# A 768-column slice of an expert table read as a stream, the other 1280 columns gathered, and a second row product per group on GpSimd

## What is computed

```
scores = einsum(q, keys)                       # 8 heads x 2 halves x 128 keys
idx, gate = top 16 of 16 x 16 sums per head    # idx = i * 128 + j, 128 experts a token
hid = gelu(einsum('td,thkd->thk', x, U[idx]))  # U: 16384 x 2048
out = einsum('thk,thkd->td', gate * hid, V[idx])
x = rms_norm(x + out)
```

## Time and profile before

| | |
|---|---|
| median of 3 runs | 2047.74 us (2046.32, 2047.74, 2051.26) |
| span of the profiled execution | 2047.2 us |
| projections | 0 to 884 us |
| first table, 63 groups after the first | 886 to 1515 us |
| tail, tile 1 | 1515 to 1564 us |
| second table and output | 1564 to 2047 us |
| busy share of the span | PE 70%, DVE 79%, ACT 42%, POOL 49% |

### The profile page before, as it was taken

How to read it: one execution, slowest core, us unless ns; L and a number is a source line. 1 busy time by engine, 2 the same in 40 slices (tenths; PEclk the granted TensorE clock), 3 DMA queues, 4 the chain that set the end, 5 groups by cost and what they waited for, 6 DMA issues and landing times.

```text
span 2047.2 us, 22565 instructions
## 1 busy us (share of the span) xinstructions
PE 1436.2 (70%) x7933; PEld 1248.8 (61%) x7933; DVE 1608.7 (79%) x1995; ACT 868.3 (42%) x1130; POOL 994.3 (49%) x699
## 2 busy tenths in 40 slices
PE   6999999999999999920000002212359999999997
PEld 6987998877888789920000001111247888888886
DVE  5465775454755556789999999977889999999998
ACT  4353443344343444311211226567856444444444
POOL 1002320000000000178888888888888788888862
PEclk9999999999999999965555555555569999999999
DMA  5555434444555555789999999999965999999996
GB/s 207 185 185 185 157 132 144 142 156 155 195 184 185 187 184 176 277 346 407 418 417 415 419 400 421 414 422 414 421 244 195 389 386 390 398 406 390 390 384 235
DMA packets 151803, 601.81 MB, mean 294 GB/s; under 512 B 14720, under 2 KB 14736, under 8 KB 118288
## 3 DMA queue, kind: packets, MB, share of 16 engines
q0 software_dynamic: 58048, 364.41, 44.0%
q1 hardware_dynamic: 93648, 236.02, 32.2%
HBM read 598.29 MB, written 2.10 MB: 293 GB/s over the span
## 4 chain that ended last, share of the span: by engine, by line
PE 55%; DVE 16%; issue 14%; POOL 7%; DMA 6%; ACT 2%; DVEq 0%; POOLq 0%; SPq 0%; ACTq 0%
PE acc L1715 7%; PE acc L1716 7%; PE acc L1717 7%; DVE slots L1470 6%; POOL slots L537 5%; PE acc L1698 4%; PE acc L1700 4%; PE acc L1701 4%; PE acc L2021 3%; PE scr L2022 3%; PE acc L2022 3%; DMA v_raw<-in_v_dense 3%; PE scr L2021 3%; PE scr L2023 3%; PE acc L2023 3%
## 5 line engine op out<-in xcount | busy, mean ns | idle before, releaser
L951 DVE TENSOR_TENSOR w_lo<-raw,w_hi 128x2048 fp32r<-128x2048 f32 x136 | 314.6, 2314 | 281.8 <-ACT w_hi L606 280.7
L1470 DVE SCALAR_TENSOR_TENSOR slots<-slots,acc 128x2048 f32<-128x2048 f32 x188 | 424.6, 2284 | 44.0 <-DMA slots<-in_peer_u,expert 41.7
L606 ACT ACTIVATE w_hi<-raw 128x2048 fp32r<-128x2048 f32 x136 | 260.1, 1913 | 409.0 <-PE acc L1717 263.3
L560 POOL DMA_INDIRECT starts<-in_v_gather,expert x256 | 365.1, 1426 | 92.9 <-DVE X L1620 77.7
L537 POOL DMA_INDIRECT slots<-in_peer_u,expert x256 | 250.2, 977 | 241.9 <-DVE expert L1442 145.2
L545 POOL TENSOR_TENSOR slots<-slots,N 128x2048 f32<-128x2048 f32 x62 | 280.5, 4524 | 37.2 <-DMA slots<-in_peer_u,expert 37.1
L887 ACT ACTIVATE v_hi<-v_raw 128x1344 fp32r<-128x1344 f32 x128 | 170.5, 1332 | 260.5 <-PE scr L2023 202.7
L800 ACT ACTIVATE slots<-slots 128x2048 f32<-128x2048 f32 x62 | 118.4, 1909 | 341.2 <-POOL slots L545 341.2
L1978 PE MATMUL scr<-hot_a,hot_b 128*128 128x128 f32 x448 | 92.4, 372 | 222.1 <-DVE hot_b L1515 158.4
L1620 DVE SCALAR_TENSOR_TENSOR X<-starts,weight,X 128x704 f32<-128x704 f32 x256 | 241.9, 945 | 0.7 <-DMA starts<-in_v_gather,expert 0.3
L1715 PE MATMUL acc<-w_hi,hT_hi 128*128 128x512 f32 x576 | 227.9, 396 | 2.5 <-DVE w_lo L951 2.5
(11 more groups left out here) (297 smaller groups left out, 3224.1 us busy)
## 6 DMA issues: line engine op xcount, KB each, us to landing
raw<-in_w_in SPq DMA_DIRECT2D x88, 1024.0 KB, 4.9
v_raw<-in_v_dense SPq DMA_DIRECT2D x128, 672.0 KB, 7.4
raw<-in_w_o SPq DMA_DIRECT2D x16, 1024.0 KB, 5.1
raw<-in_peer_wq SPq DMA_DIRECT2D x16, 1024.0 KB, 5.2
raw<-in_w_a_up SPq DMA_DIRECT2D x8, 1024.0 KB, 5.0
raw<-in_w_b_up SPq DMA_DIRECT2D x8, 1024.0 KB, 5.1
slots<-in_peer_u,expert POOLq DMA_INDIRECT x256, 9.6
starts<-in_v_gather,expert POOLq DMA_INDIRECT x256, 8.0
```

What stands on the lines that cost most here:

```text
L560: pool.indirect_dma_start(starts[j][:, :], None, v_gather[:, :], bass.IndirectOffsetOnAxis(ap=expert[:, s // NSEL, s % NSEL:s % NSEL + 1], ...
L606: a.activation(w_hi[:, m % 2, :, :], raw[:, m % 2, :, :], ACT.Copy).then_inc(hi_ready, 1)
L951: v.tensor_tensor(w_lo[:, m % 2, :, :], raw[:, m % 2, :, :], w_hi[:, m % 2, :, :].bitcast(fp32), ALU.subtract).then_inc(lo_ready, 1)
L1470: v.scalar_tensor_tensor(out=slots[j][:, :], in0=slots[j][:, :], scalar=1.0, in1=row, op0=ALU.mult, op1=ALU.mult, accum_out=hid_sum[:, t, ...
```

## The change

1. U is laid out as two tables: `u_gather`, the last 1280 columns, and `u_dense`, the first 768 columns in 128 blocks of 128 experts (block i holds the experts i * 128 + j), transposed for TensorE. A gather moves 128 rows of 1280 floats, and dots, products and sums cover 1280 columns.
2. In groups 0 to 31, TensorE multiplies each block by all 256 tokens: six float32 matmuls of 128x128 by 256 columns a block. ScalarE copies the results of two blocks at a time (`evict`) into the two tables weight_all[t][j, i, token], which now hold products and later the weights. `evict` for four blocks stands ahead of the `sum_product` of each group 1 to 32, and TensorE waits for the eviction of two blocks before it reuses their bank. SP loads the blocks through four buffers.
3. These tables grow over the row buffers of the gathers, so each row buffer 0 to 11 closes ahead of the eviction that overwrites it. There are 13 at the start, 6 from gather 94, 4 from 104, and 7 from 144.
4. In groups 34 to 49, four batches of four tokens a group, the right product is picked for every pick: a one-hot over j from squared distances (`squares_j` on TensorE, `hot_j` on ScalarE), a matmul against weight_all with stride (`pick`), and a maximum over i on VectorE (`find`). The row indices go through HBM (`keep_rows`, `load_rows`).
5. The one-hots of `scatter` now come from TensorE too (`squares`: eight matmuls with five rows of contraction a batch), one ScalarE pass (`hot_first`) and one VectorE pass (`hot_second`). Tile 0 has groups 50 to 63, tile 1 stands in the tail as before. VectorE takes a third of tile 1's copies. GpSimd makes no one-hots any more.
6. GpSimd multiplies two of four rows in groups 1 to 19, one from group 20 on, and none in groups 25 to 28 (VectorE has all four there).
7. X is written to HBM ahead of the first table and read back in the tail, since the picking now works in its place. The picking runs two parts a group, to group 27.

```diff
+UC = 6
+UD = UC * P
+UG = D - UD
+DVE_ALONE = range(100, 116)
+TWO_BEFORE = 80
+SELECT_FROM, SELECT_END = 34, 50
...
 def on_pool(q):
-    return q % FOUR == FOUR - 1 and FOUR <= q < GATHERS - 1
+    if q % FOUR == 1 and FOUR <= q < TWO_BEFORE:
+        return True
+    return q % FOUR == FOUR - 1 and FOUR <= q < GATHERS - 1 and q not in DVE_ALONE
...
+def row_open(j, q):
+    if j < HELD_ROW:
+        return q < 2 * overwritten(j) - 4 and (q >= FOUR or j in FIRST_ROWS)
+    if j == HELD_ROW:
+        return FOUR <= q < P
+    return q >= (60 if j in SCORE_ROWS else 112 if j in ALL_ROWS else 144)
...
+            def load_u(m):
+                if m < 2:
+                    sp.wait_ge(scr_ready[half_of("dense1")], use_number("dense1"))
+                elif m < len(UB_AT):
+                    sp.wait_ge(unit_done, UNIT0[G_END])
+                else:
+                    sp.wait_ge(u_used, m - len(UB_AT) + 1)
+                n = m % len(UB_AT)
+                sp.dma_start(ubs[n][:, :], u_dense[:, P - 1 - m, :]).then_inc(u_landed[n], 16)
...
-                if q == 2 * FOUR:
+                if q == FOUR:
                     pool.wait_ge(unit_done, UNIT0[G_END])
+                    pool.wait_ge(scr_ready[1], use_number("score3"))
...
             for n in range(GROUPS):
                 for q in range(FOUR * n, FOUR * n + FOUR):
                     gather(q)
-                if on_pool(FOUR * n - 1):
-                    product(FOUR * n - 1)
+                for q in range(max(0, FOUR * n - FOUR), FOUR * n):
+                    if on_pool(q):
+                        product(q)
...
+            def evict(u):
+                act.wait_ge(u_used, 2 * u + 2)
+                for j in range(HELD_ROW):
+                    if overwritten(j) == u:
+                        wait_rows(act, j)
+                bank = dense_bank[u % 2].rearrange("p (b t s) -> p b t s", b=2, t=NT)
+                for t in range(NT):
+                    last = a.activation(weight_all[t][:, P - 2 - 2 * u:P - 2 * u, :], bank[:, :, t, :], ACT.Copy)
+                last.then_inc(evicted, 1)
...
             for i in range(GROUPS):
+                if 0 < i <= GROUPS // 2:
+                    evict(2 * i - 2)
+                    evict(2 * i - 1)
+                for b in selected(i):
+                    hot_j(b)
...
+                for q in range(FOUR * i, FOUR * i + FOUR):
+                    if on_pool(q):
+                        sum_product(q)
...
+            for m in range(BLOCKS):
+                n, u = m % len(UB_AT), m // 2
+                if m % 2 == 0 and u >= 2:
+                    pe.wait_ge(evicted, u - 1)
+                pe.wait_ge(u_landed[n], 16 * (m // len(UB_AT) + 1))
+                to = dense_bank[u % 2][:, (1 - m % 2) * S:(2 - m % 2) * S]
+                for k in range(UC):
+                    last = t_.matmul(to, ubs[n][:, k * P:(k + 1) * P], h2Tf[:, k, :], start=k == 0, stop=k == UC - 1)
+                last.then_inc(u_used, 1)
...
+            def pick(b):
+                room, g5 = row_group(b)
+                if b >= 2:
+                    pe.wait_ge(hid_found, b - 1)
+                t, n, to = b // BATCHES, b % BATCHES, picked[b % 2]
                 for c in range(SC):
+                    t_.matmul(to[:, c * P:(c + 1) * P], room[g5, c * P:(c + 1) * P], tests_i[g5, :], start=c == 0, stop=False,
+                              skip_group_check=True)
+                for c in range(SC):
+                    last = t_.matmul(to[:, c * P:(c + 1) * P], hot_a[:, b % 2, c, :], weight_all[t][:, :, n * SC + c],
+                                     start=False, stop=c == SC - 1, skip_group_check=True)
+                last.then_inc(picked_ready, 1)
...
+            for w in range(BATCHES, NT * BATCHES):
+                if w + 1 < NT * BATCHES:
+                    squares(w + 1)
+                scatter(w)
```

More of the change, by code:

```diff
@@ new lines, in row_table, with first_use, selected @@
+def row_table():
+    last, table = [-GATHERS + j for j in range(len(ROW_AT))], []
+    for q in range(GATHERS):
+        j = min((j for j in range(len(ROW_AT)) if row_open(j, q)), key=lambda j: last[j])
+        last[j] = q
+        table.append(j)
+    return table
+ROW_OF = row_table()
+def buffer_of(q):
+    return ROW_OF[q]
+def uses_before(q, j):
+    return sum(SEM_OF[r] == SEM_OF[j] for r in ROW_OF[:q])
+def first_use(q):
+    return ROW_OF[q] not in ROW_OF[:q]
+def selected(i):
+    if not SELECT_FROM <= i < SELECT_END:
+        return range(0)
+    per = NT * BATCHES // (SELECT_END - SELECT_FROM)
+    return range(per * (i - SELECT_FROM), per * (i - SELECT_FROM + 1))
@@ L160, in start_at, with spread, parts, evictor @@
+def spread(i):
+    if i < SPREAD_FROM:
+        return range(0)
+    n = GROUPS - SPREAD_FROM
+    return range(BATCHES * (i - SPREAD_FROM) // n, BATCHES * (i - SPREAD_FROM + 1) // n)
+def parts(i):
+    return range(min(56, 2 * i), min(56, 2 * i + 2))
+def evictor(w):
+    n = w - BATCHES
+    return "dve" if n >= 0 and (n % 3 == 2 or n == BATCHES - 1) else "act"
+def evictions(w, by):
+    return sum(evictor(v) == by for v in range(w))
 def start_at(s):
     return s % CRING if s < WIDE_FROM else (s - WIDE_FROM) % (2 * CRING)
+def start_count(s):
+    rows = sum(SEM_OF[r] == start_at(s) for r in ROW_OF)
+    return 16 * (rows + len(starts_before(s)) + 1)
@@ new lines, in squares @@
+            def squares(w):
+                room, g5 = row_group(NT * BATCHES + w)
+                if w:
+                    pe.wait_ge(a_ready, w)
+                for c in range(SC):
+                    last = t_.matmul(square_a[:, c * P:(c + 1) * P], room[g5, c * P:(c + 1) * P], tests_i[g5, :],
+                                     start=True, stop=True)
+                last.then_inc(a_squared, 1)
+                if w:
+                    pe.wait_ge(b_hot_ready, w)
+                for c in range(SC):
+                    last = t_.matmul(square_b[:, c * P:(c + 1) * P], room[g5, c * P:(c + 1) * P], tests_j[g5, :],
+                                     start=True, stop=True)
+                last.then_inc(b_squared, 1)
@@ new lines, in scatter @@
+            def scatter(w):
+                t = w // BATCHES
+                before = w - 1 if w <= BATCHES else w - 2 if w > BATCHES + 1 else None
+                if w and before is not None:
+                    pe.wait_ge(scattered[evictor(before)], evictions(before + 1, evictor(before)))
+                pe.wait_ge(a_ready, w + 1)
+                pe.wait_ge(b_hot_ready, w + 1)
+                for c in range(SC):
+                    last = t_.matmul(scatter_bank[w % 2 if t else 0][:, c * P:(c + 1) * P], hot_b[:, w % 2, c, :],
+                                     hot_a[:, w % 2, c, :], start=True, stop=True)
```

517 lines of the change are left out of this document (305 added, 212 removed).

## The result

The changed kernel takes 2209.86 us (median of 4 runs, 2206.1 to 2213.67), the kernel before 2047.45 us beside it (4 runs, 2046.32 to 2051.26). The ratio is 1.0787, with a 95% interval of 1.0769 to 1.0805: **slower by 162 us**, far outside the range. The profiled execution has a span of 2207.8 us, 161 us above that of before.

A forecast was written before the change was run, and what follows sets the result against it. In the first table it took DMA bytes, DVE and POOL to be all close to full. Terms 4 + 19 + 6 + 5 - 19 - 21 + 28 gave +22 us, so 2070 us, range 2025 to 2122 us.

The forecast's parts named there:

- I take the full clock for it: TensorE in groups 0 to 31: full clock assumed, 24 float32 matmuls a group at 0.43 us, 10.3 us.
- a clock of 0.5 in the picking: One of the listed signs that would show the forecast wrong: TensorE at half clock while picking products.
- the clock falls: Rival: TensorE at half clock in the picking, 3.6 us a batch, 15.5 a group, +110, 2180 us; chance 0.05.
- Groups 33 to 49: Picking in the first table: fewer bytes, ScalarE's list couples four batches, 9.0 us a group, -19 us.
- the hand-over: Between block evictions and picking: row indices load and one batch passes before the first `find` returns, +5 us (0 to 10).
- the first rival: Strided picks cost 0.86 ns an element, picking groups take about 11.8 us, +45 us, 2115 us; chance 0.20.
- Tail: Behind the first table: TensorE makes one-hots in line, 2.15 us a batch against 1.28, 32 batches, +28 us.
- The second rival: Five-row small matmuls cost next to nothing, a tail batch stays at 1.35 us, 2026 us in all; chance 0.20.
- Groups 50 to 63: Later first-table groups, with tile 0's weight batches: 8.6 us a group, -1.5 x 14 = -21 us.
- Groups 1 to 19: First-table groups with two POOL products: POOL's list of products and gather issues binds at 11.1 us, +19 us.
- Groups 20 to 32: First-table groups with one POOL product or none: bytes 10.6 and TensorE 10.3 bind, +6 us.
- Start and second table: Start: gathers from the fifth on wait for the last scores, +4 us; second table: unchanged work at the DMA's limit, nothing.

The follow-up runs named there:

- the control: The change with each batch's rows alone in a zero-filled buffer (six buffers), still five rows, and second-table and X loads behind the last batches: 2245.36 us.
- the early load: The kernel with 128-row small matmuls, plus the first block of the second table loaded while the scatter runs: 2103.72 us, ratio to before 1.027.
- the filled kernel without stride: The change plus six more full 128-row matmuls in every batch of picks and scatter, with picks reading neighbouring elements: 2315.27 us, timed once.

## Why the prediction was wrong

- **The step that failed** is the clock: "I take the full clock for it, since it had that in every stretch in which it was as busy". It held for groups 1 to 32 (0.98 from 900 to 1200 us), whose matmuls have 128 rows, and I carried it into the picking and the tail, whose small matmuls have five. The stretches of before with a busy TensorE that I had looked at hold matmuls of full height. What the runs showed in its place is 0.50 at 50.00 of 50 us busy, and 1.00 once the small matmuls have 128 rows, worth 135 us against the control. The prediction's own sign of being wrong, a clock of 0.5 in the picking, is what came.
- **The rival "the clock falls"** was the right one and got 0.05, on the same ground: "It would have to stay low while TensorE is the bound and hence busy". It was low with 50.00 of 50 us busy. Its 2180 us missed 2210 by errors that partly cancel: it priced a batch of picks at 3.6 us and a group at 15.5 (measured 3.07 and 13.0; side by side the small matmuls save 0.42 of it), and it left out the groups 50 to 63 and the tail, where a batch at half clock takes 3.90 us.
- **Groups 33 to 49** (-14 with the hand-over, measured +48.3). With 128 rows it is +13.9 (185.9 against 172.0), and without the stride too -7.5 (164.4). So the clock cost most, then the first rival, the stride: priced at 0.86 ns an element, measured 0.72, but only visible at full clock. The remaining 6.5 us stay open.
- **Tail** (+28, measured +88.5). The price of a batch was right for the clock assumed, with its parts a little off: 2.12 us in the few microseconds at full clock against 2.15, namely 1.03 for the small matmuls with their changes of height (priced 1.2) and 1.09 for the old four (priced 0.97). The sum left out that three batches of tile 0 still come after the last dot: in the change the first batch of tile 1 starts 13.9 us behind it (1601.04), before it was 5.0 us (1519.83). With 128 rows and the early load the tail is +29.2 (78.4 against 49.2), but that it meets the forecast is luck, since its batches take 1.79 us, which is +16. The second rival, small matmuls next to free, is out: by either clock they take half of a tail batch.
- **Groups 50 to 63** (-21, measured -6.2): -16.9 with 128 rows, so most of the miss is the clock again.
- **Groups 1 to 19** (+19, measured +12.0). GpSimd's list had no room, but at 10.66 us and not 11.1: two products of 2.9 need no hand-over between them. The groups took 10.4 us on the mean, and before 9.8 (185.7 / 19), not 10.1, so two errors partly cancel. The 7 us that its second product costs were real and of no use to remove.
- **Groups 20 to 32** (+6, measured +12.9), 11.0 us each, within the bounds of 10.3 to 11.2. I had bytes and TensorE bind; gathers also waited for row buffers. Groups 1 to 32 together took 10.6 us each (340.2 / 32), the prediction's price by bytes, and the two terms add up to 25 against 24.9: the sum is right, the split is not.
- **Start and second table**: +4 and 0, measured +5.4 and -0.2.

The sign stood; the assumption about TensorE's clock cost the range. With the rows changed, the time came to 2104 to 2111 us, and without the stride (same work, other numbers) to 2088, 18 us above the forecast of 2070.

## What to carry to other kernels

Here a busy TensorE was not a TensorE at full clock: before pricing a stretch at full clock, look at whether its matmuls use all 128 rows, and give a stretch with few-row matmuls both prices. Where indices or flags can be padded with zero rows for nothing, a taller matmul cost no more here (a tail batch of 1.79 us with 128 rows, 1561.50 to 1563.29, against 2.12 with five, both at full clock) and brought the clock back. At full clock the moving operand read with a stride was dear (1.60 against 0.86 us for eight passes), at half clock it was not (2.03 against 2.00), so one fault can hide the other.

## What was not expected of the hardware

- Granted clock 0.50 with PE busy 50.00 of 50 us, for 5, 32 and (in the picking) 64 rows; 1.00 for 128 rows, 123 of them zero.
- Two matmuls on different groups of 32 rows started at the same instant (1300.11), worth 0.42 us a batch.
- The stride of 512 bytes: 0.72 ns an element at full clock, 2.03 against 2.00 us for eight passes at half clock.
- With the same work a stretch stood at 0.50 and at 1.00 in one execution (the filled kernel without stride).
